# Differential attention: the second map scaled on GpSimd, transposes three steps behind, two value tiles and the out-projection parts at other steps

## The reference, cut to what matters

```python
s = jnp.einsum('bqhcd,bkhcd->bhcqk', q, k) * DIFF_HEAD_DIM ** -0.5
p = jax.nn.softmax(s, axis=-1)
w = p[:, :, 0] - lam * p[:, :, 1]
o = jnp.einsum('bhqk,bkhe->bqhe', w, v)
o = rms_norm(o, subln_gain) * (1.0 - lam_init)
return o.reshape(b, l, D_MODEL) @ w_out
```

## Time and profile before

| | us |
|---|---|
| median of the runs shown | 1194.96 |
| the profiled execution's own time | 1191.34 |
| its span, first to last instruction | 1189.6 |
| TensorE busy | 1150.6 (97%) |
| VectorE busy | 740.7 (62%) |
| ScalarE busy | 556.5 (47%) |
| GpSimd busy | 130.9 (11%) |
| attention loop, first scores to first sum into x | 622.89 to 684.06 |

### The profile page before, as it was taken

One profiled execution on the slowest core, in us unless ns is written; L12 is line 12 of the kernel. 1 busy time (PEld: TensorE's weight loads), 2 busy tenths in 40 slices (PEclk: granted clock), 3 DMA queues, 4 the chain that ended last, 5 costly groups with the idle time before them and its releaser, 6 DMA issues.

```text
span 1189.6 us, 18840 instructions
## 1 busy us (share of the span) xinstructions
PE 1150.6 (97%) x7088; PEld 966.6 (81%) x7088; DVE 740.7 (62%) x1236; ACT 556.5 (47%) x1058; POOL 130.9 (11%) x185
## 2 busy tenths in 40 slices
PE   8999999999999999999998999999999999999898
PEld 6665787877878888778995799999998887899666
DVE  5764566766733333578769696445568596645773
ACT  4453322222223232456447675444556676567662
POOL 0012011122200000212100110000010000132410
PEclk8999999999999999999999999999999999999999
DMA  8999356578732332223340155555553444164320
GB/s 281 376 336 323 130 163 195 170 252 278 263 107 72 107 106 72 70 72 106 107 143 1 36 173 182 182 195 188 176 152 107 139 145 133 53 200 142 110 72 35
DMA packets 121672, 182.85 MB, mean 154 GB/s; under 512 B 4497, under 2 KB 92896, under 8 KB 121600
## 3 DMA queue, kind: packets, MB, share of 16 engines
q1 hardware_dynamic: 113888, 154.44, 39.4%
q0 software_dynamic: 7712, 27.43, 7.1%
HBM read 180.48 MB, written 1.05 MB: 153 GB/s over the span
## 4 chain that ended last, share of the span: by engine, by line
PE 80%; DVE 10%; ACT 5%; issue 4%; POOL 1%; DVEq 0%; ACTq 0%; POOLq 0%
PE ps L528 20%; PE ps L530 20%; PE ps L529 20%; PE ps L966 2%; PE ps L968 2%; PE ps L967 2%; DVE wl L510 2%; PE ps L2607 1%; ACT wh L503 1%; DVE hl L737 1%; DVE nrm L721 1%; PE ps L2975 1%; PE ps L2977 1%; PE ps L2976 1%; PE ps L1223 1%
## 5 line engine op out<-in xcount | busy, mean ns | idle before, releaser
L510 DVE TENSOR_TENSOR wl<-raw,wh 128x1024 fp32r<-128x1024 f32 (+1 forms) x246 | 297.5, 1214 | 224.2 <-ACT wh L503 221.1
L528 PE MATMUL ps<-hh,wh 128*128 128x256 f32 (+3 forms) x1272 | 418.0, 329 | 7.6 <-DVE hl L737 2.8
L529 PE MATMUL ps<-hl,wh 128*128 128x256 f32 (+3 forms) x1272 | 414.0, 325 | 0.0
L530 PE MATMUL ps<-hh,wl 128*128 128x256 f32 (+3 forms) x1272 | 413.1, 325 | 0.0
L503 ACT ACTIVATE wh<-raw 128x1024 fp32r<-128x1024 f32 (+1 forms) x246 | 252.5, 1032 | 261.2 <-PE ps L530 249.6
L528 PEld LDWEIGHTS ps<-hh,wh 128*128 128x128 f32 x1272 | 239.6, 188 | 47.6 <-issue 14.8
L530 PEld LDWEIGHTS ps<-hh,wl 128*128 128x128 f32 x1272 | 240.0, 189 | 21.0
L529 PEld LDWEIGHTS ps<-hl,wh 128*128 128x128 f32 x1272 | 239.0, 188 | 20.2
L528 PE MATMUL ps<-ah,wh 128*128 128x256 f32 (+2 forms) x376 | 126.1, 335 | 2.7 <-DVE big L1128 1.5
L529 PE MATMUL ps<-al,wh 128*128 128x256 f32 (+2 forms) x376 | 124.2, 330 | 0.0
L530 PE MATMUL ps<-ah,wl 128*128 128x256 f32 (+2 forms) x376 | 124.2, 330 | 0.0
(11 more groups left out here) (298 smaller groups left out, 1530.6 us busy)
## 6 DMA issues: line engine op xcount, KB each, us to landing
raw<-in_ffn_w_in SPq DMA_DIRECT2D x44, 1024.0 KB, 5.2
raw<-in_ffn_w_out SPq DMA_DIRECT2D x22, 1024.0 KB, 5.0
raw<-in_w_in SPq DMA_DIRECT2D x22, 1024.0 KB, 5.4
big<-in_w_ada SPq DMA_DIRECT2D x16, 1024.0 KB, 10.6
big<-in_w_ada POOLq DMA_DIRECT2D x24, 512.0 KB, 4.5
ex<-in_w_ada POOLq DMA_DIRECT2D x24, 512.0 KB, 5.1
raw<-in_diff_w_in SPq DMA_DIRECT2D x12, 1024.0 KB, 5.2
raw<-in_w_out SPq DMA_DIRECT2D x8, 1024.0 KB, 5.0
```

Source lines behind the costliest of these rows:

```text
L510: ins = nc.vector.tensor_tensor(place(wl), v, place(wh).bitcast(F32), ALU.subtract)
L528: nc.tensor.matmul(o, w_hi, m_hi, start=first, stop=False, **kw)
L529: nc.tensor.matmul(o, w_hi, m_lo, start=False, stop=False, **kw)
L530: return nc.tensor.matmul(o, w_lo, m_hi, start=False, stop=last, **kw)
```

## The change

On GpSimd `heads_split` becomes `second_maps`: for each step it waits for the inverse sums (a new semaphore, s_rc) and scales the second map in place; VectorE's L1353 goes, and its combination moves one iteration back (step i - 2 in iteration i) and waits for GpSimd (s_second_map). The high and low parts of head f are made in GpSimd's iteration 2 f + 7, behind that iteration's scaling. On TensorE the transposes are of step i - 3, directly behind the scores, then comes the tail, and then the values' product or the sum of squares. On ScalarE the copy of step i - 3 stands ahead of the exponentials. Two value tiles instead of one are left for the attention loop, in iterations 2 and 3. The out-projection parts m = 0 to 3 stand in iterations 16, 17, 18 and 19, and m = 0 and 1 wait for the exponentials up to step 14 alone.

```diff
 def att_pe(pe, a, tail, late_unit):
-                if i == 2:
-                    last_unit()
+                if i in (2, 3):
+                    late_unit(i - 2)
                 if i < a["steps"]:
                     ...  # scores
+                if 3 <= i < a["steps"] + 3:
+                    j0 = i - 3
+                    pe.wait_ge(s_w, a["s0"] + j0 + 1)
+                    ...  # waits as before, four transposes
+                tail(i)
                 if i % 2 == 1 and 0 <= (i - 5) // 2 < a["heads"]:
                     ...  # values' product
                 if a["name"] == "diff" and i % 2 == 0 and 0 <= (i - 6) // 2 < a["heads"]:
                     sub_sum(pe, a, (i - 6) // 2)
-                if 2 <= i < a["steps"] + 2:
-                    j0 = i - 2
-                    ...  # the transposes
-                if tail:
-                    tail(i)
 def att_act(act, link, a, last_unit):
-                if i == 2:
-                    units_act(act, link, last_unit, False)
+                if i in (2, 3):
+                    units_act(act, link, DIFF_UNITS[i - 4:][:1], False)
                 if i == a["steps"]:
                     round_next(act, last_unit[0]["q"] - 1, 2)
+                if 3 <= i < a["steps"] + 3:
+                    j0 = i - 3
+                    ...  # copy of the transposed weights, ahead of the exponentials
                 if i < a["steps"]:
                     ...  # exponentials
-                if 2 <= i < a["steps"] + 2:
-                    j0 = i - 2
-                    ...  # the copy
+        def second_maps(pool, a):
+            for i in range(a["steps"] + 8):
+                if i < a["steps"]:
+                    j = i % a["deep"]
+                    pool.wait_ge(s_rc, i + 1)
+                    part = a["ex"][:, j, 1, 0:a["keys"]]
+                    nc.gpsimd.tensor_scalar(part, part, rc[:, j, 1:2], sml[:, 5:6], ALU.mult, ALU.mult)\
+                        .then_inc(s_second_map, 1)
+                f, odd = divmod(i - 6, 2)
+                if odd and 0 <= f < a["groups"] - 1:
+                    pool.wait_ge(s_on, a["g0"] + f + 1)
+                    ...  # high and low part of head f, as in heads_split
 def att_dve(dve, link, mark, a, last_unit):
                 if i < a["steps"]:
                     ...  # row maxima
                 if 1 <= i <= a["steps"]:
-                    if diff:
-                        inverted = inverse(i - 1)
-                    weights(i - 1, inverted)
+                    j = (i - 1) % deep
+                    dve.wait_ge(s_ex, a["m0"] + i * a["maps"])
+                    nc.vector.reciprocal(rc[:, j, 0:a["maps"]], sm[:, j, 0:a["maps"]]).then_inc(s_rc, 1)
+                if 2 <= i <= a["steps"] + 1:
+                    j = (i - 2) % deep
+                    dve.wait_ge(s_second_map, i - 1)
+                    nc.vector.scalar_tensor_tensor(out=exp[:, j, 0, 0:n], in0=exp[:, j, 0, 0:n],
+                                                   scalar=rc[:, j, 0:1], in1=exp[:, j, 1, 0:n],
+                                                   op0=ALU.mult, op1=ALU.add).then_inc(s_w, 1)
 # in the three callers, units_pe, units_act, units_dve:
-            units_pe(pe, DIFF_UNITS[:-1], BASE["diff"])
+            units_pe(pe, DIFF_UNITS[:-2], BASE["diff"])
 def diff_tail(i):
-                for m in {steps + 1: (0, 1), steps + 3: (2,), steps + 4: (3,)}.get(i, ()):
-                    pe.wait_ge(s_ex, ATT["diff"]["maps"] * steps)
+                m = i - steps
+                if 0 <= m < 4:
+                    pe.wait_ge(s_ex, ATT["diff"]["maps"] * (steps - 1 + m // 2))
                     outproj_part(pe, diff_out[m], m, range(5), L, head_split)
```

More of the change, by code:

```diff
@@ L440, in build @@
         s_hr = sem("head_rounded_by_pool")
+        s_rc = sem("sums_inverted")
+        s_second_map = sem("second_map_scaled")
         s_bias = sem("bias_ready")
@@ L1225, in att_pe @@
                     ins.then_inc(s_sc, 1)
+                if 3 <= i < a["steps"] + 3:
+                    j0 = i - 3
+                    pe.wait_ge(s_w, a["s0"] + j0 + 1)
+                    if j0 == 0:
+                        bank_free(pe, DIFF_UNITS[:-1], 4)
+                    if j0 == 1:
+                        pe.wait_ge(s_ucp, 16)
+                    positive(pe, s_trc, a["s0"] + j0 - 1)
+                    for j, (at, n) in enumerate(chunk_plan(a["keys"])):
+                        ins = nc.tensor.transpose(ps[0:n, 4 + j0 % 2, j * P:(j + 1) * P],
+                                                  a["ex"][:, j0 % a["deep"], 0, at:at + n], T["ident"])
+                    ins.then_inc(s_tr, 1)
+                tail(i)
                 if i % 2 == 1 and 0 <= (i - 5) // 2 < a["heads"]:
@@ L1294, in att_act @@
                     ins.then_inc(s_trc, 1)
+                if i < a["steps"]:
+                    for c in range(a["maps"]):
+                        act.wait_ge(s_mx, a["s0"] + i + 1)
+                        src = ps[:, score_bank(a, i, c), 0:a["keys"]]
+                        r = i % a["deep"]
+                        if i >= a["deep"]:
+                            act.wait_ge(s_tr, a["s0"] + i - a["deep"] + 1)
+                        nc.scalar.activation(a["ex"][:, r, c, 0:a["keys"]], src, ACT.Exp,
+                                             bias=nm[:, r, c:c + 1],
+                                             accum_out=sm[:, r, c:c + 1]).then_inc(s_ex, 1)
                 if diff and i % 2 == 1 and 0 <= (i - 5) // 2 < a["heads"]:
@@ L1329, in o_split @@
                                     ALU.subtract).then_inc(s_os, 1)
[L1331 to L1338, removed]
+        def second_maps(pool, a):
+            for i in range(a["steps"] + 8):
+                if i < a["steps"]:
+                    j = i % a["deep"]
[6 more added lines that the diff above has]
+                    pool.wait_ge(s_on, a["g0"] + f + 1)
+                    nc.gpsimd.tensor_copy(o_out(a, f, hh), o_scaled(a, f)).then_inc(s_hr, 1)
+                    pool.wait_ge(s_hr, f + 1)
+                    nc.gpsimd.tensor_tensor(o_out(a, f, hl), o_scaled(a, f), o_out(a, f, hh).bitcast(F32),
+                                            ALU.subtract).then_inc(s_os, 1)
         def att_dve(dve, link, mark, a, last_unit):
@@ L1366, in att_dve @@
                     dve.wait_ge(s_sc, a["s0"] + i + 1)
-                if 1 <= i <= a["steps"] and not diff:
-                    inverted = inverse(i - 1)
-                if i < a["steps"]:
                     b = score_bank(a, i, 0)
```

22 lines of the change are left out of this document (5 added, 17 removed).

## The result

The changed kernel takes 1199.61 us (median of 8 runs, 1198.77 to 1201.82), the kernel before 1194.15 (8 runs, 1190.26 to 1195.08): the ratio is 1.0056, 95% interval 1.0042 to 1.0070, so it is slower by 5 to 8 us. The profiled execution took 1199.27, 7.9 more than that of the kernel before; its span is 1196.8, 7.2 more.

What follows compares the result with a forecast made beforehand. TensorE (27.0 of 29.5 us busy) and VectorE (27.4) bound the attention loop. Start +0.4, steady loop -2.6, loop's end +5.7 give +3.5 us: 1194.8 from the profiled execution, 1198.5 with 3.6 to the median; range 1195.2 to 1201.2.

Steps and rivals of the forecast that it cites:

- Part 1: Attention loop's start: the two value tiles after the first scores leave the first gap unfilled; 0.4 us lost.
- S(0): Scores of step 0 on TensorE, the loop's first; forecast to go from 622.89 to 620.05.
- S(2): Scores of step 2 on TensorE, forecast to wait 2.4 us for step 0's exponentials.
- Part 2: Steady loop: scaling moves from VectorE to GpSimd, a pair of steps takes 5.5 us; 2.6 us won.
- Rival B: Steady loop: GpSimd wins the shared port each time, delaying even steps' combinations; +4.8 us, 1199.8, chance 0.12.
- Part 3: Loop's end: first out-projection part waits for head 4's low part, behind the last scaling; 5.7 us lost.
- X: Start of the last scores, those of step 15, on TensorE; forecast at 662.8 against 664.98.
- W: Time at which GpSimd has written the low part of head 4; forecast X + 9.25 us.
- granted clock 1.00 over both: Sign expected in the new trace: TensorE's clock stays full over the start's 2.4 us wait and the tail's 4 us wait.
- rival C: TensorE's long gaps: its clock falls, 5 us of dense work at half speed; +6.0 us, 1201.0, chance 0.10.
- A: Tail rival: slab splits come after head 4's cast and subtraction; last part costs 3.7, sum +1.5 us, 1196.5, chance 0.15.
- D: Tail rival: head 4's low part is there when TensorE asks; -0.7 us, 1194.3, not slower, chance 0.13.

Runs made afterwards that it cites:

- e1: Changed kernel with idle products filling TensorE's two long gaps, ahead of the scores of step 2 and before head 4's products; ratio 1.0043 to the kernel before.
- e10: A repeat of e5, unchanged, on another chip; ratio 0.9952 to the kernel before.
- e7: Changed kernel with VectorE's two slab splits at the loop's end in iteration 19 instead of 17; ratio 1.0039 to the kernel before.
- e2: Changed kernel with GpSimd making a head's parts ahead of the scaling, not behind it; ratio 1.0015 to the kernel before.
- e5: Changed kernel with one value tile in the loop, head parts ahead of the scaling, out-projection parts in iterations 16, 17, 20, 21; ratio 0.9956 to the kernel before.
- e3: Changed kernel with the out-projection parts in iterations 17, 18, 20 and 21 instead of 16 to 19; ratio 1.0025 to the kernel before.
- e6: Changed kernel with the scaling of the second map on VectorE again; ratio 1.0050 to the kernel before.
- e8: Kernel of e5 with two value tiles left for the loop instead of one; ratio 0.9984 to the kernel before.
- e4: Changed kernel with one value tile left for the loop, in iteration 2; ratio 1.0034 to the kernel before.
- e11: Kernel of e5 with the scaling of the second map on VectorE, run again for a profile; ratio 1.0006 to the kernel before.

## Why the prediction was right, and where not

The forecast was +3.5 us, 1198.5, with a range to 1201.2; measured were 1199.61 and a ratio whose interval begins above what can be told from no change. The direction, the place and the wait were right. The size was short by the clock. That the time itself came within 1.1 us is in part luck: 3.6 us of the 1198.5 are the distance of a median of three runs from the profiled execution, and beside the experiments the kernel before had medians of 1191.1 to 1193.8 instead of 1194.96. Profile against profile the change is +7.9 us, more than twice the forecast.

**Part 1, the start.** The timeline of TensorE in the changed kernel, S(0), S(2), S(3), S(6):

```profile
618.16 1.99 PE L1225 MATMUL ps<-big 64*128 64x512 f32 x8
...
625.48 1.51 PE L1225 MATMUL ps<-big 64*128 64x512 f32 x4 [2.31 <-ACT big L1293]
...
631.10 1.13 PE L1225 MATMUL ps<-big 64*128 64x512 f32 x4
...
638.45 1.13 PE L1225 MATMUL ps<-big 64*128 64x512 f32 x4
```

VectorE's first reduction begins at 622.72, S(0) + 4.56 (4.57 forecast), and the gap ahead of S(2) is 2.31 us (2.4 forecast). From then on S(2) takes 1.51 instead of 1.13 us and the second tile's first products 0.21 apart instead of 0.12. At full clock (e1) the start takes 15.92 us, +0.5 on the kernel before, where +0.4 was forecast. With the clock it is +2.0.

**Part 2, the steady loop.** A pair takes 5.49 us (5.5 forecast), S(6) to S(15) 24.05 (24.1 forecast). The old pair was 6.0 us from S(6) to S(14), and not the 5.9 that the prediction took by dividing 26.7 by four and a half; its sum doesn't use that figure. VectorE and GpSimd in one pair:

```profile
657.32 0.73 DVE L1368 SCALAR_TENSOR_TENSOR big<-big,rc 128x512 f32<-128x512 f32 x1
...
657.50 1.19 POOL L1339 TENSOR_SCALAR big<-big,rc,sml 128x512 f32<-128x512 f32 x1 [1.96 <-DVE rc L1364]
...
658.64 0.39 POOL L1344 CAST hh<-nrm 128x256 fp32r<-128x256 f32 x1
...
659.12 0.73 POOL L1346 TENSOR_TENSOR hl<-nrm,hh 128x256 fp32r<-128x256 f32 x1
...
659.40 1.00 DVE L1368 SCALAR_TENSOR_TENSOR big<-big,rc 128x512 f32<-128x512 f32 x1
...
659.84 1.20 POOL L1339 TENSOR_SCALAR big<-big,rc,sml 128x512 f32<-128x512 f32 x1
```

In the even step the combination of 657.32 is at its own 0.73 us, and the scaling, begun 0.18 later, takes 1.19: VectorE had the port first. The shortest scaling of the loop takes 0.765 us, beside no two-input instruction; 0.75 was the forecast. In the odd step the combination of 659.40 meets GpSimd's subtraction (659.12 to 659.85) and takes 1.00: it ends 0.55 after it, as in the earlier trace rows. I hadn't listed this second meeting, and it costs nothing, since the transposes of that step come later. These rows show the exclusive lock that the prediction cites from the Trainium skill, page SBUF — State Buffer, section "SBUF: two separate sides", in both directions: the second to come ends 0.55 us (VectorE) or 0.64 us (GpSimd) after the first. Rival B didn't happen: the combination of the even steps keeps its 0.73 us.

**Part 3, the tail.** The wait and what makes it:

```profile
662.50 1.13 PE L1225 MATMUL ps<-big 64*128 64x512 f32 x4
...
667.25 1.19 POOL L1339 TENSOR_SCALAR big<-big,rc,sml 128x512 f32<-128x512 f32 x1 [0.71 <-DVE rc L1364]
...
668.20 2.64 DVE L512 TENSOR_TENSOR wl<-raw,wh 128x1024 fp32r<-128x1024 f32 x2 [0.41 <-ACT wh L505]
668.38 1.38 POOL L1344 CAST hh<-nrm 128x256 fp32r<-128x256 f32 x1
...
669.85 1.57 POOL L1346 TENSOR_TENSOR hl<-nrm,hh 128x256 fp32r<-128x256 f32 x1
...
671.48 0.58 PE L530 MATMUL ps<-hh,wh 128*128 128x256 f32 x1 [3.46 <-POOL hl L1346]
...
685.75 0.70 PE L1261 MATMUL ps<-sq,tab 128*128 128x256 f32 x2 [0.47 <-ACT sq L1300]
...
688.96 0.38 PE L530 MATMUL ps<-hh,wh 128*128 128x256 f32 x1 [1.80 <-DVE hl L1329]
...
689.61 0.48 DVE L2343 SCALAR_TENSOR_TENSOR x_lat<-ps,ada,x_lat 128x256 f32<-128x256 f32 x1 [0.71 <-PE ps L532]
```

X is 662.50. The scaling of step 15 ends at X + 5.9 (6.0 forecast), the first slab split begins at X + 5.7, the cast of head 4 takes 1.38 us and its subtraction 1.57 with their waits for the port, and W is 671.42, X + 8.9 (9.25 forecast). TensorE stood 3.46 us and went on with head 4's products. The waits for the last squares (0.47) and the last low part (1.80, about 2.4 forecast) are there as well. With full clock (e1) the tail takes 24.46 us, +5.4 where +5.7 was forecast.

**The step that failed** is the last of the list of what would show it: "granted clock 1.00 over both". It was put apart as rival C, at 0.10, and priced at +2.5 us. In truth it came on top of the forecast at both gaps, 1.5 us behind the one of 2.3 us and 2.65 behind the one of 3.5 us. The gaps of up to 1.2 us of the kernel before, on which I let it rest, bear on shorter waits than those I had just worked out. With the clock kept at 1.00 (e1) the sum holds: the loop costs +3.3 us, +3.5 was forecast.

**The median.** Added to the loop's 7.4 us come +1.7 in the rest and -1.9 before the loop, both places without any changed instruction. The kernel before varies by itself from 1189.2 to 1195.7 us over its runs on one chip or another, and with the clock: of the 17 beside e10, eleven took at most 1192.1 us at a mean clock of 0.993 to 0.996, six 1194.0 to 1195.6 at 0.991 or 0.992. So a forecast of the median to better than 2 us was not to be had from one profile.

**The rivals.** A (the splits after head 4's parts) is not what happened. e7 makes it so by moving the splits: W comes at X + 7.4 (7.3 in A), but with the clock's falls the tail is still +5.4 us and not A's +3.7. D is e2: with head 4 there in time the loop costs +0.8 us, where -0.7 at full clock was worked out; the fall of the clock at the start, 1.5 us, is the difference. So the changed kernel, mended in that one place, is still not faster, and it takes the tile and the placement of the parts too (e5).

## What to carry to other kernels

Work that is moved to an idle engine goes ahead of everything already in that engine's list: ask which later user waits for the item behind it, here the split of one head behind the last scaling, and turn the order where the old item is ready first. Filler work (a value tile, out-projection parts) is worth something only in front of a wait: move it earlier and the gap opens where it was. After a forecast of a gap, price what TensorE's clock does behind it, on top and not as another case: here 1.5 us behind a gap of 2.3 us and 2.65 behind one of 3.5. Behind waits of 0.9 to 2.25 us it fell in some executions and not in others, at up to 3.0 us a place.

## What the runs showed of the hardware

- The clock fell behind the gap of 2.3 us ahead of S(2) in all six profiles that have it unfilled (changed kernel, e2, e3, e6, e7, e8), and behind the one of 3.5 us in the tail in both (changed kernel, e4). Behind the last wait of 1.8 us it fell in e6 and e7 (0.90 and 0.81 in 684 to 690 us), and not in the changed kernel, e1, e2 and e4. In e7 it fell behind the 1.9 us for head 4 as well (0.83 and 0.74 in 668 to 676); it didn't behind the 1.6 us of e3.
- Behind the same gap of 2.25 us, between 915 and 929 us, it fell in the changed kernel, e1, e2, e3, e4 and e11, and not in both profiles of the kernel before, e5, e6, e7, e8 and e10. From the first sum to a wait of 0.90 us near 1150 us the first six take 464.4 us; of the others e6 and e7, which are still slow from the last wait of the loop, take 463.8, the rest 462.8.
- Shorter waits are not safe either. Near 1150 us every kernel has a wait of 0.90 and one of 1.07 us, 1.7 us apart. In e1, e2 and e4 the clock fell there, in the ten other profiles it stayed at 1.00. Only e3 shows a fall behind a wait of 1.71 us near 1110 us (0.90 and 0.68 in 1108 to 1116), which the others have too, and lost nothing that the stretches show. The timeline and a window of e2 behind the waits of 0.90 and 1.07 us:

```profile
1148.80 0.44 PE L1591 MATMUL ps<-tab,ex 128*128 128x128 f32 x2 [0.90 <-DVE ex L1675]
1150.52 1.12 PE L1609 MATMUL ps<-x_ctx 112*64 112x256 f32 x4 [1.07 <-ACT x_ctx L1642]
...
1152.00:1154.00 2.00, 2.00 (x12) 1.50 (x9) 1.16 (x3) 1.37 (x4) 0.00 (x0) 0.50 0.87 328
```

- From the wait of 0.90 us to the end of the span e1 takes 44.2 us, e2 and e4 45.7, all others 42.7 or 42.8. These places make up the spread of the rest, 505.5 to 510.1 us; the profiled executions of e2 and e4 are also the slowest of their runs. What decides whether the clock falls is open.
- GpSimd's scaling of 128 x 512 float32 with two per-partition factors takes 0.765 us alone and 1.19 when VectorE's two-input instruction got the port 0.18 us earlier. On VectorE the same takes 0.53 to 0.55, 0.58 from start to start.
- Two-input VectorE work of 1.2 us apiece made GpSimd's passes of 0.40 and 0.73 us last 1.3 to 1.6 us in both places where the two were put side by side (changed kernel: head 4; e7: head 5). The slab splits in turn took 2.64 and 2.55 us for the pair instead of 2.35.
